# Local attention: which engine copies the turned probability tiles out of PSUM

## What is computed

```python
def row_block(args):                       # one row of 64 queries, all 6 heads
    q_r, rs, dr = args
    k_band = lax.dynamic_slice_in_dim(kg, rs, win_h, axis=2)      # 8 rows of keys
    v_band = lax.dynamic_slice_in_dim(vg, rs, win_h, axis=2)
    k_win = k_band[:, :, :, col_idx]                              # 16 columns near each query
    v_win = v_band[:, :, :, col_idx]
    s_loc = jnp.einsum('bhcd,bhrckd->bhcrk', q_r, k_win) * scale + bias
    s_ctx = jnp.einsum('bhcd,bhjd->bhcj', q_r, kch) * scale       # 256 context keys
    p = jax.nn.softmax(jnp.concatenate([s_loc, s_ctx], axis=-1), axis=-1)
    return einsum(p_loc, v_win) + einsum(p_ctx, vch)
```

## Time and profile before

| what | value |
|---|---|
| three runs before | 3109.62, 3113.05, 3114.88 us (median 3113.05) |
| the profiled execution, its own time | 3113.23 us |
| its span in the trace | 3111.4 us |
| granted TensorE clock, mean of the span | 0.993 of full speed |
| TensorE (PE) matmul busy | 2998.3 us, 96% |
| VectorE (DVE) busy | 1454.1 us, 47% |
| ScalarE (ACT) busy | 827.4 us, 27% |
| GpSimd (POOL) busy | 1280.3 us, 41% |

### The profile page before, as it was taken

How to read it: one execution, slowest core, us unless ns; L and a number is a source line. 1 busy time by engine, 2 the same in 40 slices (tenths; PEclk the granted TensorE clock), 3 DMA queues, 4 the chain that set the end, 5 groups by cost and what they waited for, 6 DMA issues and landing times.

```text
span 3111.4 us, 41011 instructions
## 1 busy us (share of the span) xinstructions
PE 2998.3 (96%) x16710; PEld 2451.0 (79%) x16710; DVE 1454.1 (47%) x1845; ACT 827.4 (27%) x1142; POOL 1280.3 (41%) x637
## 2 busy tenths in 40 slices
PE   7999998999999999999989999999999999999999
PEld 5887876788877787777767888777888888888877
DVE  3154418428725422924777402453662144144457
ACT  2141215302234122511566411114310011001252
POOL 2232220026652333036663444456743333443663
PEclk9999999999999999999999999999999999999999
DMA  6210111333231011113321111114411111111422
GB/s 243 85 35 15 41 31 49 114 116 136 65 136 41 15 36 50 60 67 95 122 88 41 48 48 51 41 53 137 142 54 51 50 47 47 47 48 48 149 75 81
DMA packets 69299, 225.54 MB, mean 72 GB/s; under 512 B 8608, under 2 KB 10400, under 8 KB 69152
## 3 DMA queue, kind: packets, MB, share of 16 engines
q1 hardware_dynamic: 47712, 162.55, 16.5%
q10 hardware_dynamic: 21440, 60.87, 5.3%
HBM read 206.62 MB, written 16.78 MB: 72 GB/s over the span
## 4 chain that ended last, share of the span: by engine, by line
PE 67%; issue 12%; DVE 8%; POOL 6%; DMA 4%; ACT 2%; POOLq 0%; SPq 0%; ACTq 0%; DVEq 0%
PE ps L643 59%; DMA raw<-s 3%; DVE Sb L2272 3%; POOL w_hi L543 3%; POOL w_lo L547 3%; PE ps L955 2%; PE ps L869 1%; DMA sinT<-ropes 1%; PE ps L787 0%; PE ps L875 0%; DVE g_lo L2689 0%; PE ps L891 0%; PE ps L846 0%; DVE st L2274 0%; DVE ST L2217 0%
## 5 line engine op out<-in xcount | busy, mean ns | idle before, releaser
L543 POOL TENSOR_TENSOR w_hi<-raw,pool_zero 128x1024 fp32r<-128x1024 f32 (+2 forms) x298 | 533.4, 1792 | 1733.7 <-PE ps L643 1639.5
L547 POOL TENSOR_TENSOR w_lo<-raw,w_hi 128x1024 fp32r<-128x1024 f32 (+2 forms) x298 | 712.1, 2392 | 22.0
L643 PE MATMUL ps<-g_hi,w_hi 128*128 128x512 f32 x1696 | 569.0, 395 | 17.8 <-DVE xc L2619 5.7
L643 PE MATMUL ps<-g_lo,w_hi 128*128 128x512 f32 x1696 | 562.3, 391 | 0.0
L643 PE MATMUL ps<-g_hi,w_lo 128*128 128x512 f32 x1696 | 539.6, 390 | 1.8 <-POOL w_lo L547 1.8
L643 PE MATMUL ps<-h_hi,w_hi 128*128 128x512 f32 (+1 forms) x1496 | 418.2, 371 | 2.5 <-DVE Y L2303 1.4
L643 PE MATMUL ps<-h_lo,w_hi 128*128 128x512 f32 (+1 forms) x1496 | 407.8, 364 | 0.0
L643 PE MATMUL ps<-h_hi,w_lo 128*128 128x512 f32 (+1 forms) x1496 | 394.8, 364 | 2.3 <-POOL w_lo L547 2.3
L643 PEld LDWEIGHTS ps<-g_hi,w_hi 128*128 128x128 f32 x1696 | 318.7, 188 | 94.8 <-issue 8.5
L643 PEld LDWEIGHTS ps<-g_hi,w_lo 128*128 128x128 f32 x1696 | 319.1, 188 | 69.6 <-POOL w_lo L547 2.6
L643 PEld LDWEIGHTS ps<-g_lo,w_hi 128*128 128x128 f32 x1696 | 319.7, 188 | 66.7 <-issue 0.5
(11 more groups left out here) (393 smaller groups left out, 3353.5 us busy)
## 6 DMA issues: line engine op xcount, KB each, us to landing
raw<-s SPq DMA_DIRECT2D x263, 512.0 KB, 3.5
modring<-modw ACTq DMA_DIRECT2D x32, 512.0 KB, 4.5
modfirst<-modw SPq DMA_DIRECT2D x4, 1024.0 KB, 18.0
modfirst<-modw ACTq DMA_DIRECT2D x4, 1024.0 KB, 24.7
x_saved<-Y ACTq DMA_DIRECT2D x1, 4096.0 KB, 15.1
x_part<-x_saved ACTq DMA_DIRECT2D x2, 2048.0 KB, 9.2
x_saved<-Y ACTq DMA_DIRECT2D x2, 2048.0 KB, 8.7
B<-x_saved ACTq DMA_DIRECT2D x1, 4096.0 KB, 14.0
```

Source lines behind the costliest of these rows:

```text
L543: last = G.tensor_tensor(hi, weights, none, ALU.add)
L547: last = G.tensor_tensor(lo, weights, hi.bitcast(F32), ALU.subtract)
L643: last = T.matmul(ps[:, o + c0:o + c0 + size], wt[s][:, k * P:(k + 1) * P], xx[:, k, t0:t0 + size], start=(x == 0 and n == 0), stop=(x == ...
```

## The change

Bank 5 is copied by ScalarE too, between its two other copies. VectorE copies nothing. The semaphore `pt_dve` goes, and TensorE waits for `pt_act` alone. `groups_before(l, i, 0, 1)` counts all groups of the units before i, three for each token unit and one for each context unit. The whole diff is short:

```diff
@@ TensorE
                     tiles = key_tiles(i, t)
-                    ga, gd = groups_before(l, i, 0, 2), groups_before(l, i, 1, 2)
+                    ga = groups_before(l, i, 0, 1)
                     for x, (a, _, p) in enumerate(tiles):
                         if x == 0 or a != tiles[x - 1][0]:
                             pe.wait_ge(p_ready, 2 * (ub + i) + a + 1)
                         if x == 0 and ga:
                             pe.wait_ge(pt_act, ga)
-                        if x == 4 and gd:
-                            pe.wait_ge(pt_dve, gd)
...
-                    pe.wait_ge(pt_act, groups_before(l, i + 1, 0, 2))
-                    pe.wait_ge(pt_dve, groups_before(l, i + 1, 1, 2))
+                    pe.wait_ge(pt_act, groups_before(l, i + 1, 0, 1))
@@ ScalarE
                 def turned(i):
 
-                    for g in range(0, turned_groups(units[i][1]), 2):
-                        n = 4 if g == 0 else 2
+                    for g in range(turned_groups(units[i][1])):
+                        n = 4 if g < 2 else 2
                         o = (4 + g) * BANK
                         act.wait_ge(pt_ready, groups_before(l, i, 0, 1) + g + 1)
                         if g == 0 and ub + i:
                             act.wait_ge(pv_ready, ub + i)
                         A.activation(turned_tile(4 * g, n), ps[:, o:o + n * P], ACT.Copy).then_inc(pt_act, 1)
@@ VectorE
-                def turned(i):
-
-                    if units[i][1] < QT:
-                        dve.wait_ge(pt_ready, groups_before(l, i, 0, 1) + 2)
-                        if ub + i:
-                            dve.wait_ge(pv_ready, ub + i)
-                        V.tensor_copy(turned_tile(4, 4), ps[:, 5 * BANK:6 * BANK]).then_inc(pt_dve, 1)
...
                     sums(i)
-                    turned(i)
                     if i:
                         place(i - 1)
```

More of the change, by code:

```diff
@@ L338, in build_kernel @@
         s_ready, nm_ready = sem("s_ready"), sem("nm_ready")
-        p_ready, pt_ready, pt_dve, pt_act = sem("p_ready"), sem("pt_ready"), sem("pt_dve"), sem("pt_act")
+        p_ready, pt_ready, pt_act = sem("p_ready"), sem("pt_ready"), sem("pt_act")
         rinv_ready, pv_ready, y_used = sem("rinv_ready"), sem("pv_ready"), sem("y_used")
```

## The result

The change makes the kernel slower, by about the 6.5 us that the forecast has.

| | before | after |
|---|---|---|
| median | 3113.09 us | 3119.65 us |
| lowest to highest | 3109.62 to 3116.27 us | 3115.94 to 3122.70 us |
| ratio after / before, 95% interval | | 1.0020, 1.0013 to 1.0027 |

A forecast was written before the change was run, and what follows sets the result against it. TensorE is busy 96% of the span; VectorE's ring paces steady attention units at 4.32 us, ScalarE's follows at 4.06. With the added copy ScalarE's sets 39 turns: +6.5 us on 3113.23 gives 3119.7 us, range 3113.5 to 3124.

The forecast's parts named there:

- full turn of ScalarE's ring: Local attention, token unit: copies, head 1's exponential, turning, `apply`, next copies; 4.06 us plus 0.50 gives 4.56, above VectorE's 4.32.
- turn that ends at a context tile: Local attention, from a unit's copies to those of a context tile: 3.42 us plus 0.50 gives 3.92.
- pair 0: First pair of units in layer 0's attention: 11.86 us becomes 13.04, two full turns and one ending at a context tile.
- last `apply`: End of the attention stages: it waits for three copies instead of VectorE's place, 1.52 against 1.37 us, +0.15.
- The ten intervals: Units of both stages where VectorE also sets bias zeros: 4.68 us apart, at most 0.35 us each to gain.
- The price of the third copy: ScalarE's added 512-column copy: 0.50 us start to start, bounds 0.27 and 0.60.
- What is late next: Behind ScalarE's copies: the turning, `apply`, `pv_ready`, then the following copies, each turn 0.24 us more until 4.56 us.
- The turns that count: Both attention stages: 39 turns of ScalarE's ring lengthen, together +6.5 us.
- Bias loads in pair 0 absorb what came earlier: Layer 0, early units of the first pair: they wait for a load of biases, which absorbs their delay.
- B: Rival, attention stages: third copy adds under 0.26 us, VectorE's freed time gives back 3.5 us, 3109.7 us; chance 0.09.
- C: Rival, ScalarE: the third copy costs its full 0.60 us, 3.9 us more, 3123.6 us; chance 0.13.
- D: Rival, TensorE's clock: a drop at a pair boundary, or none, moves 1.5 us; 3118.2 to 3122.7 us; chance 0.16.

The follow-up runs named there:

- vector_busy: The kernel after, with an unused maximum over 512 columns on VectorE where its copy was; 3118.77 us, ratio 1.0022 to before.
- no_bank5: The kernel before, with VectorE's copy of bank 5 left out in all but each layer's first unit; 3108.91 us, ratio 0.9985 to before.
- wide_copy: The kernel after, with banks 4 and 5 copied by one ScalarE instruction of 1024 columns; 3116.20 us, ratio 1.0013 to before.
- bank_waits: The kernel after, with the turning waiting for each bank's own copy instead of all three; 3120.15 us, ratio 1.0022 to before.
- exp_third: The kernel after, with waits for each bank and head 1's exponential ahead of the copy of bank 6; 3113.11 us, ratio 0.9999 to before.
- more_copy: The kernel after, with one more unused 256-column ScalarE copy in each token unit; 3135.86 us (4 runs), ratio 1.0070 to before.
- exp_second: The kernel after, with waits for each bank and head 1's exponential right behind the copy of bank 4; 3114.73 us, ratio 1.0003 to before.
- third_wide: The kernel after, with banks 4 and 5 in one ScalarE copy, then head 1's exponential, then bank 6; 3110.90 us, ratio 0.9995 to before.

## Why the prediction was right

The forecast was 3119.7 us, measured were 3119.65. That they agree so closely is partly luck: the interval of the difference is 4 us wide, and the trace itself has 6.04 us where the sum had 6.51. Its terms, one by one:

| term | forecast | trace |
|---|---|---|
| full turn of ScalarE's ring | 4.56 us | 4.55 us |
| turn that ends at a context tile | 3.92 us | 3.91 us |
| pair 0 | 13.04 us, +1.18 | 13.01 us, +1.15 |
| pair 1 | 31.28 us, +1.49 | 31.21 us, +1.42 |
| pair 2 | 31.28 us, +1.47 | 31.21 us, +1.40 |
| layer 1, 22 turns | 100.32 us, +2.22 | 100.13 us, +2.03 |
| last `apply` | +0.15 us | +0.04 us |
| sum | +6.5 us | +6.04 us |

- **VectorE's copy is off the path in steady units, and its removal buys nothing after the change.** Right: vector_busy puts it back in length and changes the stages by 0.47 us. For the removal alone the forecast had at most 3.5 us; no_bank5 shows 4.25. The ten intervals gave back 0.25 us each on the mean, less than the 0.35 taken, because loads of biases land just behind; two other intervals and the last `apply` gave back the rest.
- **The price of the third copy.** 0.50 taken, 0.49 measured (4.55 less 4.06). That the step and not the duration counts was the choice that mattered most, and wide_copy confirms the small fixed part. By the full duration the sum would have been 3123.6 us.
- **What is late next.** Right: the exponential of head 1, then the middle of the turning (2.23 us after the copies in the forecast, 2.22 in the trace), `apply`, and the next copies. bank_waits excludes the banks: with the same waits exp_third moves the exponential ahead of the last copy and takes 7.5 us from the stages. Not as forecast is the chain of waits: it also runs through VectorE's head-1 maximum and the scores, which end together with the ring of ScalarE.
- **The turns that count.** Right at this price. more_copy shows how soon the count would have been wrong: with 0.30 us more in a turn the stages grow as by 45 turns, not 39.
- **The last `apply`.** Sized too large: I took the 0.14 us between the copies and the turning for the delay behind them, but `apply` starts 1.41 us after the copies start, against 1.37 us before.
- **Bias loads in pair 0 absorb what came earlier.** Right in effect: from the second unit's scores to the first copies in the sum it is 26.98 us in before and 26.95 in after, and the sum of layer 0 has no term besides the three pairs (1.15 + 1.42 + 1.40 = 3.97 of 3.96).

Of the rivals, B (the ring does not bind) is excluded by the 4.55 us and by more_copy. C (full duration) is excluded by the step of 0.49. D (the clock) is no cause of the 6.04 us. A drop appears in five of the eleven profiled executions: at the pair boundary in before and no_bank5 (1.5 us each), in the last turn of layer 1 in more_copy (1.4 us), at the end of the stage of layer 0 in exp_second and third_wide (0.7 and 0.6 us), and in neither profile of after in the stages. The forecast took the profiled execution of before, which has such a drop, as its base and left the drop in. That after's has none is one reason why the two spans are only 3.7 us apart; the medians of 14 runs hang less on such luck.

Of the two rules of the Trainium skill, the advice to use both ScalarE and VectorE for evacuating PSUM (TensorEngine Tiling (Array Packing), "PSUM Bottleneck") held here for this order of instructions: one engine alone cost 6 us. But exp_third, with ScalarE alone and another order, has shorter stages than before. By the table of the Trainium skill (VectorE: DVE Perf Modes, "The TRN2 errata") the copy would cost 570 ns and the change 9.2 us, an estimate, which lies above the interval of 4.0 to 8.4 us of the 14 runs; a step of 0.49 us is what the traces show.

## What to carry to other kernels

An engine that is busy for half of a stage can still have no room, if its instructions stand in a ring of waits: write down each ring with its lengths, and price an added instruction against the ring with the least margin, here 0.26 us. In an engine's list, ask what is queued behind the instruction that waits; moving one 256-column copy behind the exponential was worth more (7.5 us in the stages) than giving the whole copy back to the other engine. And price an instruction in a queue by the step to the next start, not by its duration in the profile.

## What the runs showed of the hardware

ScalarE's copies of fp32 from PSUM follow each other faster than their durations say: 512 columns have a duration of 0.59 us and a step of 0.49. One instruction of 1024 columns instead of two of 512 saved only 0.05 to 0.06 us. A copy of 256 columns with PSUM as its destination stepped 0.31 us, and one to SBUF 0.26 (1256.85 to 1257.11 in more_copy), so the destination in PSUM wasn't faster. TensorE's granted clock dropped to half in some profiled executions and not in others of the same order. In before it did at the pair boundary near 542 us, behind a wait of 1.61 us, and not near 500 us in the same execution, behind one of 1.62 us. In more_copy it was down during the `apply` at 1351.03, one turning after a wait of 1.91 us; the same place of after, behind a wait of 1.61 us, ran at the full level. What decides it stays open.
